# Eight of sixteen head slabs multiplied as high and low parts: a two-layer hybrid block on one NeuronCore

## What is computed

```
cond = jax.nn.silu(c)
mod = (cond @ ada_w[layer] + ada_b[layer])[:, None, :]
sh_m, sc_m, g_m, sh_f, sc_f, g_f = jnp.split(mod, 6, axis=-1)
h = rms_norm(x, norm_w[layer, 0]) * (1.0 + sc_m) + sh_m
u = h @ w_in
```

## Time and profile before

| | us |
|---|---|
| median of 3 runs | 2513.05 |
| lowest and highest | 2510.29, 2514.41 |
| the profiled execution | 2513.01 |
| its span | 2511.2 |
| TensorE, VectorE, ScalarE busy in the span | 2417.5, 1911.0, 1005.7 |
| end of the last head matmul in the span | 153.13 |

### The profile page before, as it was taken

One profiled execution on the slowest core, in us unless ns is written; L12 is line 12 of the kernel. 1 busy time (PEld: TensorE's weight loads), 2 busy tenths in 40 slices (PEclk: granted clock), 3 DMA queues, 4 the chain that ended last, 5 costly groups with the idle time before them and its releaser, 6 DMA issues.

```text
span 2511.2 us, 39774 instructions
## 1 busy us (share of the span) xinstructions
PE 2417.5 (96%) x15930; PEld 2218.6 (88%) x15930; DVE 1911.0 (76%) x2355; ACT 1005.7 (40%) x1028; POOL 427.0 (17%) x200
## 2 busy tenths in 40 slices
PE   7999989899999999999999999998999999999998
PEld 5888887699988999799879889987999899989996
DVE  5769987789978998789877766677666766666665
ACT  2134544353333333333445544444433333333343
POOL 0000000024410432034100000000344024411430
PEclk8999999999999999999999999999999999999999
DMA  9989966847788777877858543475555765576553
GB/s 363 414 343 361 358 241 233 304 180 274 276 304 314 273 273 287 311 280 277 303 196 299 209 151 142 145 251 202 185 184 184 286 219 182 183 260 243 184 184 134
DMA packets 114472, 627.14 MB, mean 250 GB/s; under 512 B 12768, under 2 KB 12960, under 8 KB 63152
## 3 DMA queue, kind: packets, MB, share of 16 engines
q1 hardware_dynamic: 113648, 621.22, 67.3%
q10 hardware_dynamic: 704, 4.23, 0.5%
HBM read 623.27 MB, written 2.13 MB: 249 GB/s over the span
## 4 chain that ended last, share of the span: by engine, by line
PE 78%; DVE 13%; DMA 6%; ACT 3%; issue 1%; DVEq 0%; ACTq 0%; SPq 0%
PE bank L1721 16%; PE bank L1722 16%; PE bank L1723 16%; PE bank L1746 7%; PE bank L1748 7%; PE bank L1747 7%; DMA piece<-ada_pieces 5%; DVE lo L934 5%; PE bank L1526 4%; DVE piece L945 3%; ACT hi L506 2%; PE bank L1633 1%; PE bank L1505 1%; DVE y L945 1%; PE bank L1538 1%
## 5 line engine op out<-in xcount | busy, mean ns | idle before, releaser
L506 ACT ACTIVATE hi<-raw 128x2048 fp32r<-128x2048 f32 x378 | 723.4, 1914 | 1159.7 <-PE bank L1723 716.6
L1721 PE MATMUL bank<-act,hi 128*128 128x256 f32 x3616 | 1029.9, 285 | 6.8 <-DVE lo L934 4.7
L1722 PE MATMUL bank<-act,hi 128*128 128x256 f32 x3616 | 1024.3, 283 | 0.0
L1723 PE MATMUL bank<-act,lo 128*128 128x256 f32 x3616 | 1024.2, 283 | 0.0
L934 DVE TENSOR_TENSOR lo<-raw,hi 128x2048 fp32r<-128x2048 f32 x378 | 864.9, 2288 | 165.0 <-ACT hi L506 164.1
L1721 PEld LDWEIGHTS bank<-act,hi 128*128 128x128 f32 x3616 | 695.2, 192 | 11.5 <-DVE lo L934 6.4
L1722 PEld LDWEIGHTS bank<-act,hi 128*128 128x128 f32 x3616 | 695.3, 192 | 0.2
L1723 PEld LDWEIGHTS bank<-act,lo 128*128 128x128 f32 x3616 | 695.0, 192 | 0.0
L945 DVE SCALAR_TENSOR_TENSOR piece<-piece,cond 128x1024 f32<-128x1024 f32 x290 | 398.6, 1378 | 76.7 <-DMA piece<-ada_pieces 76.6
L915 POOL TENSOR_TENSOR region<-region 128x256 f32<-128x256 f32 x88 | 205.2, 2331 | 1021.3 <-ACT region L817 1021.3
L1746 PE MATMUL bank<-hi,mid 128*128 128x512 f32 x704 | 276.7, 393 | 10.8 <-DVE lo L934 10.7
(11 more groups left out here) (178 smaller groups left out, 1689.3 us busy)
## 6 DMA issues: line engine op xcount, KB each, us to landing
raw<-w_units SPq DMA_DIRECT2D x378, 1024.0 KB, 4.9
piece<-ada_pieces SPq DMA_DIRECT2D x290, 512.0 KB, 5.1
region<-ada_pieces SPq DMA_DIRECT2D x64, 512.0 KB, 11.2
raw<-head_units SPq DMA_DIRECT2D x16, 1024.0 KB, 12.4
y<-ada_pieces SPq DMA_DIRECT2D x30, 512.0 KB, 6.5
region<-gamma_scratch ACTq DMA_DIRECT2D x4, 1024.0 KB, 7.4
x<-x_in SPq DMA_DIRECT2D x1, 2048.0 KB, 9.2
x_out<-x SPq DMA_DIRECT2D x3, 512.0 KB, 2.8
```

The source lines that it names most:

```text
L506: sc.activation(hi[:, slot, :], raw[:, raw_slot, :], ACT.Copy).then_inc(s_hi, 1)
L1721: pe.matmul(dst, w_hi, act[:, kt, 0:T], start=at == 0, stop=False)
L1722: pe.matmul(dst, w_hi, act[:, kt, T:2 * T], start=False, stop=False)
L1723: i_ = pe.matmul(dst, w_lo, act[:, kt, 0:T], start=False, stop=at == DK - 1)
```

## The change

A table names eight slabs, 4, 5, 7, 8, 10, 11, 13 and 14. For these ScalarE, after it has made the activations of the round, waits for the slab in `raw` and copies it to one of the two `hi` slots; VectorE, after `head_low(kt - 1)`, subtracts into `lo`; and TensorE multiplies the slab in three products instead of one fp32 product, for which it also waits for `head_low(kt)` (`s_hact`). The other eight slabs are multiplied as before. The copy of the first projection unit now also waits for slab 14.

```
+HEAD_SPLIT = (4, 5, 7, 8, 10, 11, 13, 14)
...
                     sc.activation(act[:, kt, 0:T], y[:, kt, :], ACT.Copy).then_inc(s_hhi, 1)
+                    if kt in HEAD_SPLIT:
+                        u = HEAD_SPLIT.index(kt)
+                        sc.wait_ge(s_raw[kt % RAW_SLOTS], 16 * (kt // RAW_SLOTS + 1))
+                        if u >= SPLIT_SLOTS:
+                            sc.wait_ge(s_slab, HEAD_SPLIT[u - SPLIT_SLOTS] + 1)
+                        sc.activation(hi[:, u % SPLIT_SLOTS, :], raw[:, kt % RAW_SLOTS, :], ACT.Copy).then_inc(s_slab_hi, 1)
+                sc.wait_ge(s_slab, HEAD_SPLIT[-1] + 1)
                 split(0, 0, 0, HEAD_USES + 1)
...
                         head_low(kt - 1)
+                    if kt in HEAD_SPLIT:
+                        u = HEAD_SPLIT.index(kt)
+                        slot = u % SPLIT_SLOTS
+                        ve.wait_ge(s_slab_hi, u + 1)
+                        ve.tensor_tensor(lo[:, slot, :], raw[:, kt % RAW_SLOTS, :], hi[:, slot, :].bitcast(F32),
+                                         ALU.subtract).then_inc(s_slab_lo, 1)
                 head_low(DK - 1)
...
                     pe.wait_ge(s_hn, kt + 1)
+                    if kt in HEAD_SPLIT:
+                        slot = HEAD_SPLIT.index(kt) % SPLIT_SLOTS
+                        pe.wait_ge(s_slab_lo, HEAD_SPLIT.index(kt) + 1)
+                        pe.wait_ge(s_hact, kt + 1)
+                        for c in range(DK):
+                            to = bank[c // 2][:, (c % 2) * T:(c % 2 + 1) * T]
+                            w_hi, w_lo = hi[:, slot, c * P:(c + 1) * P], lo[:, slot, c * P:(c + 1) * P]
+                            pe.matmul(to, w_hi, act[:, kt, 0:T], start=False, stop=False)
+                            pe.matmul(to, w_hi, act[:, kt, T:2 * T], start=False, stop=False)
+                            i_ = pe.matmul(to, w_lo, act[:, kt, 0:T], start=False, stop=False)
+                        i_.then_inc(s_slab, 1)
+                        continue
```

More of the change, by code:

```diff
@@ L365, in program @@
         s_slab = sem("head_unit_done")
+        s_slab_hi = sem("head_unit_hi_ready")
+        s_slab_lo = sem("head_unit_lo_ready")
         s_hea = sem("head_evacuated_by_scalar")
```

## The result

| | before | after |
|---|---|---|
| median, us | 2513.26 (9 runs) | 2528.92 (9 runs) |
| lowest, highest | 2508.14, 2519.26 | 2523.40, 2535.32 |
| ratio, 95% interval | | 1.0063, 1.0049 to 1.0076 |
| span of the profiled execution | 2511.2 | 2525.7 |
| slab 0 multiplied (slab 4's load is issued) | 49.56 | 46.08 |

The account below looks back on a forecast made before the run. TensorE's matmuls were taken to set the head's end, with DMA and VectorE nearly level. 2513.0 plus 14.1 us of later head end plus 2.2 of clock loss gave 2529.3 us, range 2526.1 to 2534.8.

Parts of the forecast that it names:

- The serial round: VectorE's subtraction waits for ScalarE's copy, itself behind alpha: split rounds take 10.54 us instead of 5.49 or DMA's 7.61.
- Round 5 and round 15: VectorE starts round 5 at 58.6 instead of 55.68 and round 15 at 148.9 instead of 134.70.
- The second wait: Split slab 14 cannot start until round 15's head_low(14), at 154.4; unsplit slab 15, 6.91 us, comes behind it.
- head_low(14) inside round 15: On VectorE, the low half of slab 14's activations is done 5.58 us after round 15 starts.
- The DMA queue: In the head, DMA has nothing to do part of the time from about round 8, so is off the path.
- The clock: TensorE's 4.8 us pause before slab 14 halves its clock afterwards, losing 2.2 us; range 0 to 5.8.
- The sum: Head ends at 167.2 instead of 153.13, 14.1 us later; clock loss adds 2.2.
- Matmul pitch: On TensorE, split-form matmuls start 0.12 us apart, so a split slab's 48 take 5.76 us against 6.91 in fp32.
- Behind the head: Unit loads, evacuation and gates after the head shift with its end as one piece, 1 us either way.
- Rival 1: TensorE's saving arrives: head ends at 148.0, time 2507.9 us; chance 0.03.
- the cover: The first projection unit's 4.2 us split, waiting for slab 14, lies beside slab 15's 6.91 us and costs nothing.

Follow-up runs that it names:

- operands alone: Changed kernel with its copies, subtractions and TensorE's wait for them kept, but all slabs multiplied in plain fp32, without waiting for low activations: 2522.02 us, 1.0038 of before.
- late subtraction: Changed kernel, eight slabs split, with VectorE subtracting each slab one round later, behind head_low(kt): 2514.73 us, 1.0009 of the kernel before.
- products with the low half: Changed kernel without copies or subtractions, hi and lo constant zeros; the wait for the activations' low half and its use stay: 2513.70 us, 0.9997 of before.
- products alone: Changed kernel without copies or subtractions, hi and lo constant zeros, activations' high half replacing the low, no head_low wait: 2514.61 us, 1.0004 of before.
- the last kernel: Kernel before, no slab split, with PSUM banks zeroed in bfloat16 and the first projection unit's load issued first: 2502.37 us, 0.9951 of before.
- the best of the split kernels: Changed kernel with only slabs 4 to 7 split, each subtracted one round later, and the first projection unit's load issued first: 2509.16 us, 0.9987 of before.
- six slabs with the unit's load first: Changed kernel with only slabs 4, 5, 7, 8, 10, 11 split, subtraction one round later, first projection unit's load issued earlier: 2513.24 us, 1.0000 of before.

## Why the prediction was right, and where not

Predicted 2529.3, measured 2528.92. Step by step, measured from the end of slab 0 so that the early clock drops out:

- *The serial round.* Predicted 10.54 us for a split round and 5.49 for an unsplit one; measured 10.43 to 10.44 and 5.49, one split round (11) 10.75. VectorE's wait was 2.64 or 2.65 us in all but one. The run with operands alone showed the same rounds without the products, and the run with the late subtraction showed that the order, not the work, made them. This is the step that carried the sum.
- *Round 5 and round 15.* Round 5 predicted at 58.6 - 49.56 = 9.0 after slab 0, measured 9.4; round 15 at 99.3, measured 99.3. The agreement to 0.1 is luck: the later round 5 and the long round 11 add 0.6 us, and six rounds 0.1 shorter than predicted take it away.
- *The second wait.* Predicted that head_low(14) holds slab 14; measured 151.76 to 151.90, 0.14 us apart. Its own price, products with the low half against products alone, was 5.4 us from round 15's start.
- *head_low(14) inside round 15.* Predicted 5.58 us from the round's start, measured 6.42: 0.84 short, the masks (below).
- *The DMA queue.* I wrote that DMA would have nothing to do part of the time from about round 8. Its share stayed at 1.0 until 118, in round 11. The conclusion held all the same: VectorE waited for no piece after round 4.
- *The clock.* Predicted 4.8 us of pause before slab 14 and 2.2 us lost. Measured: a pause of 5.3, half clock for 4.7 us of slab 14, and slab 14 took 159.96 - 151.90 = 8.06 us, 2.3 more than 5.76. Two windows of the pause and the slab:

```profile
149.80:151.80 2.00, 0.00 (x0) 0.00 (x0) 1.89 (x6) 0.28 (x1) 0.00 (x0) 0.50 0.46 193
151.90:156.60 4.70, 4.70 (x22) 4.70 (x23) 0.42 (x1) 0.63 (x2) 0.00 (x0) 0.50 0.00 0
```

  The size was right; the sign I read it from was not. I took the pause of 3.12 us that left the clock whole as a mark of what is harmless, and priced only the long one. But two shorter pauses, before slabs 7 and 8, were each followed by some 3 us at half clock:

```profile
87.58 0.36 PE L1549 MATMUL bank<-act,hi 128*128 128x256 f32 x1 [2.39 <-DVE act L1350]
98.02 0.36 PE L1549 MATMUL bank<-act,hi 128*128 128x256 f32 x1 [2.98 <-DVE act L1350]
```

  They cost nothing, as I had said of drops beside VectorE's rounds: they only shortened the next pause. Before slabs 7, 8, 10, 11, 13 and 14 I had 2.0, 4.8, 3.3, 4.8, 3.4 and 4.8 us; measured are 2.39, 2.98, 1.56, 4.77, 1.01 and 5.30.

- *The sum.* Predicted 16.3 us more head, measured 17.2 by head length: 0.84 from the masks, 0.1 from the clock. The medians differ by 15.7. That the total fell within half a microsecond is partly luck: the head was 0.9 us longer than predicted, the medians differ by 1.5 less than the heads, which no run explains, and the median of the kernel before itself lay between 2512.11 and 2513.31.
- *Matmul pitch.* At full clock 0.12 us, as the row had it: in round 14's stretch the third products start at 142.73 and 143.09. By the 109 ns of the Trainium skill, "TensorE: Matmul & The Clock Gate", section "Back-to-back issue gap", a slab would be 5.24 us, an estimate from 48 products. The trace disagrees: this case's units and head slabs both show 5.76.
- *Behind the head.* Predicted that it shifts as one piece. The spans differ by 14.5 and the head ends by 13.7, so 0.8 us are left, inside the 1 us given.
- *Rival 1 was priced wrongly.* I gave it 5.1 us of TensorE's 9.2, with the head's end as the only limit. Products alone had that shorter head and only 1.2 us earlier matmuls behind it, because the first unit's landing was the next thing late. The rival's 2507.9 should have been 2511.8. I named the cover for the later direction and did not ask for it in the earlier one.

Open: how much of the 0.49% of the last kernel belongs to the load order, and what makes the clock fall after one pause and not after another (below).

## What to carry to other kernels

A subtraction of 2.3 us that fits into an engine's idle time can lengthen a round by 5 us (here from 5.49 to 10.44, where DMA had set 7.6) if it stands in the queue in front of the next round's work and waits for an engine that itself waits for this one; put the consumer one round later. When an engine is said to have room, check what must be finished before its next instruction may start, not the busy share. Before pricing a shorter stage, look at what is hidden just in front of its end (here 1.2 us of room, not 5), and look at what all later times hang on: cheaper zeroing, together with one moved load, gave 9.7 us, and the best of the split kernels without it 3, which is not clear of nothing.

## What the runs showed of the hardware

- A GpSimd conversion and VectorE's two-input instructions held each other up. In the changed kernel:

```profile
144.03 2.29 POOL L889 CAST blocks<-extra 128x1024 uint8<-128x1024 f32 x1 [142.52 <-DMA extra<-blocks_in]
```

  It takes 1.04 us where VectorE is idle (145.58 in the trace before). It was issued while the subtraction at 143.13 ran, and then the piece sum at 145.34 took 2.06 us instead of 1.22. Moved away, both were back at 1.04 and 1.22. The Trainium skill, "SBUF — State Buffer", section "SBUF: two separate sides", says that a VectorE instruction with two SBUF inputs and a GpSimd instruction that reads SBUF share a port pair as an exclusive lock, and that the one that starts later blocks wholly. The numbers agree: the conversion was lengthened by 1.25 us, with 1.39 us of the subtraction left when it started, and the piece sum by 0.84, with 0.98 us of the conversion left. With slab 14 unsplit it shows again: the conversion, from 145.36 during a piece sum, took 1.68 us, and the two small mod instructions behind the sum 1.00 instead of 0.35.
- Zeroing in bf16: 8 matmuls of 512 columns in 1.88 us, against 9.5 to 12.8 for the same in fp32 in the twelve traces that have it. In fp32 the granted clock fell to half during the zeroing, between 29 and 33 us, in all twelve; with bf16 slab 0 followed at full clock in both traces.
- Pauses of TensorE and the granted clock behind them: in the head of the changed kernel, pauses of 5.30, 4.77, 2.98 and 2.39 us were followed by 0.50, those of 1.56 and 1.01 were not. The same pause, 3.12 to 3.14 us (2.93 in one trace), stands behind the first unit in all fourteen traces: in four of them, those of the two kernels among them, the clock stayed at 1.00, and in ten it was 0.50 for some us. From the changed kernel and from six slabs with the unit's load first:

```profile
182.20 0.50 PE L1775 MATMUL bank<-hi,act 128*128 128x512 f32 x1 [3.14 <-DVE lo L945]
...
165.25 0.80 PE L1777 MATMUL bank<-hi,act 128*128 128x512 f32 x1 [3.13 <-DVE lo L947]
```

  The second was followed by half clock until about 171. The length of the pause alone doesn't decide it, and I can't say what does.
